# HGRN scores of a pair of heads: one insert in the matrix engine's stream, or one insert for each head

## The reference, cut to what matters

```python
b = jnp.cumsum(lf_c, axis=-2)
decay = jnp.exp(jnp.where(causal[:, :, None], b[..., :, None, :] - b[..., None, :, :], -jnp.inf))
scores = jnp.einsum('bhtd,bhsd,bhtsd->bhts', q_c, k_c, decay)
intra = jnp.einsum('bhts,bhsv->bhtv', scores, v_c)
```

## Time and profile before

| what | us |
|---|---|
| median of three runs | 1080.36 |
| lowest and highest run | 1080.07, 1080.58 |
| the profiled execution, its own time | 1079.77 |
| its span, first to last instruction | 1078.0 |
| PE busy in the span | 1073.0 |
| DVE busy | 909.1 |
| ACT busy | 633.3 |

### The profile page before, as it was taken

The page is one execution under the profiler, slowest core; times in us unless marked ns, Lnnn a source line. Parts: engine busy times, 40 slices in busy tenths (PEclk is TensorE's granted clock), DMA queues, the critical chain, the costliest instruction groups (busy, mean ns, idle before and its releaser), DMA issues.

```text
span 1078.0 us, 18188 instructions
## 1 busy us (share of the span) xinstructions
PE 1073.0 (100%) x6543; PEld 928.2 (86%) x6543; DVE 909.1 (84%) x1376; ACT 633.3 (59%) x930; POOL 79.8 (7%) x114
## 2 busy tenths in 40 slices
PE   9999999999999999999999999999999999999998
PEld 8888888888888888888888888888898888888887
DVE  7878988979655678889888888888877889999997
ACT  7677676757544655545555555545555566656663
POOL 4500000000000000000000000000000000000000
PEclk9999999999999999999999999999999999999999
DMA  8557577777889889798888889889898789798884
GB/s 275 183 163 194 173 233 223 216 222 221 232 260 252 271 239 243 236 253 238 249 230 245 235 256 244 226 254 251 273 240 235 218 278 325 256 305 316 262 297 155
DMA packets 192336, 260.77 MB, mean 242 GB/s; under 512 B 9605, under 2 KB 143894, under 8 KB 192022
## 3 DMA queue, kind: packets, MB, share of 16 engines
q1 hardware_dynamic: 176246, 216.24, 62.2%
q0 software_dynamic: 13344, 38.80, 17.9%
q10 hardware_dynamic: 2688, 5.00, 1.2%
HBM read 255.02 MB, written 43.78 MB: 277 GB/s over the span
## 4 chain that ended last, share of the span: by engine, by line
PE 99%; DMA 1%; DVE 0%; SPq 0%; issue 0%; DVEq 0%
PE bank L1821 38%; PE bank L1829 20%; PE bank L2215 7%; PE bank L2216 7%; PE bank L2214 7%; PE bank L2067 3%; PE bank L1868 3%; PE bank L1870 3%; PE bank L2069 3%; PE bank L2068 3%; PE bank L1869 3%; PE bank L1789 1%; PE bank L1897 1%; DMA xt<-in_x_dram 1%; PE bank L2106 0%; PE bank L1986 0%
## 5 line engine op out<-in xcount | busy, mean ns | idle before, releaser
L792 ACT CAST w_hi<-raw 128x1024 fp32r<-128x1024 f32 x299 | 312.4, 1049 | 251.8 <-PE bank L1829 115.4
L1201 DVE TENSOR_TENSOR w_lo<-raw,w_hi 128x1024 fp32r<-128x1024 f32 x299 | 364.1, 1222 | 107.4 <-ACT w_hi L792 106.9
L1821 PE MATMUL bank<-hs,w_hi 128*128 128x512 f32 x1792 | 422.9, 391 | 0.0
L1821 PEld LDWEIGHTS bank<-hs,w_hi 128*128 128x128 f32 x1792 | 331.2, 188 | 66.2 <-issue 0.7
L1829 PEld LDWEIGHTS bank<-hs,w_lo 128*128 128x128 f32 x1792 | 224.5, 191 | 5.7 <-issue 0.2
L1829 PE MATMUL bank<-hs,w_lo 128*128 128x256 f32 x1792 | 227.3, 283 | 0.0
L1171 ACT CAST hi_slot<-slot 128x1024 fp32r<-128x1024 f32 (+1 forms) x102 | 117.1, 1186 | 66.2 <-DVE slot L1746 32.2
L1728 DVE TENSOR_TENSOR slot_lo<-slot,hi_slot 128x1024 fp32r<-128x1024 f32 (+1 forms) x102 | 136.6, 1388 | 5.8 <-ACT hi_slot L1171 4.7
L2216 PE MATMUL bank<-hi_slot,gated 128*128 128x512 f32 (+1 forms) x194 | 75.1, 387 | 0.0
L2214 PE MATMUL bank<-hi_slot,gated 128*128 128x512 f32 (+1 forms) x194 | 75.0, 387 | 0.0
L1646 DVE SCALAR_TENSOR_TENSOR C<-U,cols,C 128x256 f32<-128x256 f32 x176 | 73.4, 479 | 0.0
(11 more groups left out here) (248 smaller groups left out, 1184.1 us busy)
## 6 DMA issues: line engine op xcount, KB each, us to landing
raw<-in_w_ffn_up_dram SPq DMA_DIRECT2D x176, 512.0 KB, 5.1
u_sums<-in_w_ffn_down_dram POOLq DMA_DIRECT2D x58, 512.0 KB, 6.4
raw<-in_w_in_dram SPq DMA_DIRECT2D x51, 512.0 KB, 4.5
slot<-in_w_ffn_down_dram SPq DMA_DIRECT2D x38, 512.0 KB, 5.0
slot<-u_sums SPq DMA_DIRECT2D x74, 256.0 KB, 5.6
raw<-in_w_in_dram SPq DMA_DIRECT2D x66, 256.0 KB, 3.9
raw<-in_w_out_dram SPq DMA_DIRECT2D x32, 512.0 KB, 5.9
u_sums<-u_sums POOLq DMA_DIRECT2D x16, 512.0 KB, 7.1
```

The lines of the kernel that those rows point to most:

```text
L792: act.copy(w_hi[:, i, :], raw[:, i, :]).then_inc(units_hi, 1)
L1201: dve.tensor_tensor(w_lo[:, i, :], raw[:, i, :], w_hi[:, i, :].bitcast(F32), ALU.subtract)\
L1821: m = pe.matmul(banks[b][:, :], w_hi[:, i, c], hs[:, 4 * i + k, :], start=(first and k == 0), stop=(final and k == 3))
```

## The change

`head_scores` takes the head as its argument and issues the scores of this head alone: `CROSS`, then the levels from the widest to the narrowest, then `WITHIN`. `g_slot` calls it for head 0 behind the third unit, with both waits ahead of it as before, and for head 1 behind the fourth unit, with no wait ahead. Nothing else differs; the same matmuls are issued, and the counts of all semaphores are as before.

```diff
-            def head_scores():
+            def head_scores(h):
 
-                for h in range(2):
-                    tile = slice(h * P, (h + 1) * P)
-                    pe.matmul(bank_scores[h][1][:, CROSS], E[:, NL, 0, tile], E[:, NL, 1, tile],
-                              start=True, stop=True)
...
-                for l in reversed(range(NL - 1)):
-                    b, at_l = level_columns(l)
-                    for h in range(2):
-                        for t in range(TT):
...
+                tile = slice(h * P, (h + 1) * P)
+                pe.matmul(bank_scores[h][1][:, CROSS], E[:, NL, 0, tile], E[:, NL, 1, tile], start=True, stop=True)
+                for t in range(TT):
...
+                for l in reversed(range(NL - 1)):
+                    b, at_l = level_columns(l)
                     for t in range(TT):
...
+                last.then_inc(levels_made, 1)
...
-                head_scores()
+                head_scores(0)
                 unit_i_and_g(quad, 3, j, RING + 3)
+                head_scores(1)
```

More of the change, by code:

```diff
@@ L2082, in i_slot @@
                     unit_i_and_g(quad, i, j, i)
-            def head_scores():
-                for h in range(2):
-                    tile = slice(h * P, (h + 1) * P)
-                    pe.matmul(bank_scores[h][1][:, CROSS], E[:, NL, 0, tile], E[:, NL, 1, tile],
-                              start=True, stop=True)
-                for h in range(2):
+            def head_scores(h):
+                tile = slice(h * P, (h + 1) * P)
+                pe.matmul(bank_scores[h][1][:, CROSS], E[:, NL, 0, tile], E[:, NL, 1, tile], start=True, stop=True)
+                for t in range(TT):
+                    token, right = h * SEQ + t * P, (h * TT + t) * HALF
+                    b, at = level_columns(NL - 1)
+                    at += t * HALF
+                    pe.matmul(bank_scores[h][b][COLUMN_TILES[t], at:at + HALF],
+                              XK[:, NL - 1, token:token + HALF],
+                              E[:, NL - 1, 1, right:right + HALF], start=True, stop=True)
+                for l in reversed(range(NL - 1)):
+                    b, at_l = level_columns(l)
@@ L2091, in head_scores @@
                     for t in range(TT):
                         token, right = h * SEQ + t * P, (h * TT + t) * HALF
[L2093 to L2097, removed]
-                for l in reversed(range(NL - 1)):
-                    b, at_l = level_columns(l)
-                    for h in range(2):
-                        for t in range(TT):
[L2102 to L2116, removed]
+                        at = at_l + t * HALF
@@ new lines, in head_scores @@
+                        for s in COLUMN_TILES if 2 * LEVELS[l] > NARROW else NARROW_TILES:
+                            q = slice(s.start // 2, s.stop // 2)
+                            pe.matmul(bank_scores[h][b][s, at + q.start:at + q.stop],
+                                      XK[:, l, token + s.start:token + s.stop],
+                                      E[:, l, 1, right + q.start:right + q.stop], start=True, stop=True)
+                for t in range(TT):
+                    token, at = h * SEQ + t * P, WITHIN + t * P
+                    for s in NARROW_TILES:
+                        last = pe.matmul(bank_scores[h][1][s, at + s.start:at + s.stop],
+                                         KB[:, token + s.start:token + s.stop],
+                                         QB[:, token + s.start:token + s.stop], start=True, stop=True)
```

## The result

The kernel with two inserts takes 1082.04 us in the median of 22 runs, the one before 1080.37 in 22 runs. The ratio is 1.0015, with a 95% interval of 1.0009 to 1.0020. So the change costs 1.7 us, within the 0.2% that the forecast of 1082.2 called the same.

The account below looks back on a forecast made before the run. PE, busy for the whole span, was taken as the bound. Terms summed as 4 x (0.35 + 0.15) - 0.18 = +1.8 us, moving the median from 1080.36 to 1082.2 us, called the same; range 1081.0 to 1083.0.

Parts of the forecast that it names:

- Inside the inserts: Within PE's score inserts: three gaps and a restart at width changes are paid twice, +0.35 us for each pair.
- Behind the second insert: Large matmuls behind head 1's insert: the slow start behind an insert is paid once more, +0.15 us for each pair.
- The rival of the full queue: Behind the inserts: shorter runs leave PE's queue filled, both ends cost 0.09, sum +1.3 us; chance 0.14.
- The last pair's wait: Behind the last pair's insert, at L1868 and L1869: PE's wait for head 0's gather goes, -0.18 us.
- The waits laid bare: Rival, behind head 1's inserts: waits that 12 large matmuls hid would show, 0.26 us, sum +2.3; chance 0.30.
- What moves earlier is worth nothing: Head 0's scores and unit 3's follow-up work on other engines come 1.1 us earlier; PE waits for none, 0.
- The drain: At width changes in the inserts: 128 cycles, about 53 ns, would add 0.64 us; the rows' gaps, 1.2, were taken.

Follow-up runs that it names:

- head by head: Kernel before, still one insert, but head 0's whole set of scores and then head 1's behind the third unit; 1081.49 against 1079.82 us, ratio 1.0014.
- alone: Kernel before in pairs 0 to 2, with the change's two inserts in the last pair only; 1080.41 against 1079.98 us, ratio 1.0004.

## Why the prediction was right, point by point

- **Inside the inserts, +0.35 for each pair.** Measured 2 x 1.46 - 2.57 = 0.35. The sum of three gaps and a restart at the changes of width was exact. Its parts were a little off and cancelled: by the trace the stage of 64 columns with the gap behind it costs 0.12 for the 0.14 of the sum, and the stage of 32 with its end 0.14 for the 0.12. That the changes of width are the cause is shown by the pairs with one insert: with three widths the order head by head costs 0.45 us more than stage by stage (48.99 against 48.54), with one width nothing (48.20 both times).
- **Behind the second insert, +0.15.** Right in kind, too large. It is 0.12 at the second matmul, and mostly nothing after it. In three pairs the distances leave 0.43 - 0.35 = 0.08, just under the term's lower bound of 0.09. The prediction took the 0.15 of one long insert for each of two short ones. The rival of the full queue was right that both ends get cheaper, but it had 0.09 at each and so 0.03 more for a pair, too little; the 0.43 of a pair lies between its 0.38 and the forecast's 0.50. That +1.8 came so near to the medians' 1.7 is in part luck: the distances add up to 1.5, no nearer to +1.8 than to the rival's +1.3. That a queue is behind it was not shown: why the large matmuls behind some inserts run at 0.235 for several, and behind others don't, is open. It happened behind all four inserts before and behind two of the eight after, those of head 1 in the second and in the last pair.
- **The last pair's wait, -0.18.** It went, nearly in full: at the ninth matmul of the output projection the last pair costs 0.25 in the change and 0.29 alone, where another pair costs 0.43. That is 0.18 and 0.14 back.
- **The waits laid bare.** Not in three pairs: the quad f's L1821 starts 0.13 behind the last small matmul, as before. In the last pair, with four waits, the insert is 0.03 longer. If that is the rival's mechanism, it is there at about a tenth of its price of 0.26.
- **What moves earlier is worth nothing.** DVE's second gather was forecast at 177.8, which is 178.9 once the second pair's start has moved by 1.05 (172.05 to 173.10). It starts at 178.97, behind a wait of 0.27 where 0.3 was forecast. PE has no wait for it.
- **The drain.** The gaps at changes of width were taken from the rows, 0.09 to 0.12 each, and they were right: 1.45 us more inside eight inserts, the restarts included. The drain of 128 cycles that the Trainium skill states (TensorE: Matmul & The Clock Gate, Step-by-step) would, as an estimate, have given 0.64, about half of the 1.2 that the gaps alone are worth.

## What to carry to other kernels

Where PE is busy to the last slice, moving work earlier for another engine gains nothing, and every repeated change of the stationary operand's width cost 0.09 to 0.12 us here; order small matmuls by width first and by head second, or give them all one width. Before lengthening a run of small matmuls, count its instructions: of the five inserts that crossed two borders of 256 within 384 instructions, two stopped PE for 3.5 us and took the clock down with it. With 12 large matmuls between two shorter runs the same work stopped once for 0.4 us in one kernel and never in the other.

## What the runs showed of the hardware that was not expected

- A matmul of 128 stationary columns behind a stage of 32 columns pays 0.10 to 0.12 at its second record, large or small (125.34 to 125.55 head by head, where 0.11 is usual; 125.59 to 125.93 in the change, where 0.23 is usual), beside the gap of 0.12 ahead of its first.
- PE stood for 3.5 us at the second border of 256 instructions within one run of 384 small ones, in two kernels, at 320 and at 368 instructions into the run; and for 0.4 us once at such a border in a run of 192. Three other inserts with two such borders ran through. In all three stops PE went on 1.4 to 1.6 us after a 16 KB packet on the instruction queue had landed, and where an insert ran through, the packet had landed 1.8 to 2.7 us ahead of its second border. Why it came late is not settled: in the third pair it landed 4.0 us after the insert had begun, and the DMA engines were 100% busy in the window read there.
- Behind 3.5 us of idle PE the granted clock was 0.56 in the mean over the next 3.75 us, so that the 3.5 us are not the whole price of such a stop.
- Four matmuls of 32 columns side by side took less time than one of 128 or two of 64 with the changes of width that these bring: 2.15 us and an entry of 0.09 for 192 records, against 2.57 for 156.
